# Two transformer stacks on one core: values computed token by token in all layers, and the memory layers' scores as three f32r products

## What is computed

```python
# layer 0 of the first stack ("in_e"): one projection, then three attentions
z = h @ w_in_e[i]                  # queries, keys, values, gates of 8 + 8 heads of 64
a_out = nsa_attention(...)         # compressed + selected + windowed branches, 2 key/value heads
b_out = swa_sink_attention(...)    # band of 128, with sinks, 2 key/value heads

# both layers of the second stack: attention over 256 memory tokens
def memory_cross_attention(h, m, w_q, w_kv, w_o):
    q = (h @ w_q).reshape(bsz, seq, MEM_HEADS, MEM_HEAD_DIM)       # 4 heads of 256
    k, v = jnp.split(m @ w_kv, 2, axis=-1)
    s = jnp.einsum("bqhd,bkhd->bhqk", q, k) * (MEM_HEAD_DIM ** -0.5)
    p = jax.nn.softmax(s, axis=-1).astype(v.dtype)
    o = jnp.einsum("bhqk,bkhd->bqhd", p, v).reshape(bsz, seq, D_MODEL)
    return o @ w_o
```

## Time and profile before

| what | us |
|---|---|
| median of 3 runs (lowest, highest) | 2790.49 (2789.91, 2791.82) |
| the profiled execution | 2792.47 |
| its span, from first to last instruction | 2790.7 |
| PE busy in the span | 2727.5 (98%) |
| POOL, ACT, DVE busy | 1272.4, 1103.4, 1024.8 |

### The profile page before, as it was taken

One profiled execution on the slowest core, in us unless ns is written; L12 is line 12 of the kernel. 1 busy time (PEld: TensorE's weight loads), 2 busy tenths in 40 slices (PEclk: granted clock), 3 DMA queues, 4 the chain that ended last, 5 costly groups with the idle time before them and its releaser, 6 DMA issues.

```text
span 2790.7 us, 38079 instructions
## 1 busy us (share of the span) xinstructions
PE 2727.5 (98%) x13618; PEld 2232.3 (80%) x13618; DVE 1024.8 (37%) x1935; ACT 1103.4 (40%) x1796; POOL 1272.4 (46%) x713
## 2 busy tenths in 40 slices
PE   9999999999999999999999999999999999999997
PEld 7767888888867888888868888888887798888886
DVE  6664322115453322105545235222047652422202
ACT  7665332335564323223155334232237453433321
POOL 4544444444454444444435534444444463454442
PEclk9999999999999999999999999999999999999999
DMA  5301223233301222332313312322322341132231
GB/s 186 106 2 39 98 90 101 100 101 102 99 31 58 97 98 98 99 104 72 113 46 111 131 46 76 103 92 98 105 84 93 103 151 46 61 113 98 91 108 65
DMA packets 69221, 252.06 MB, mean 90 GB/s; under 512 B 7680, under 2 KB 7936, under 8 KB 68864
## 3 DMA queue, kind: packets, MB, share of 16 engines
q1 hardware_dynamic: 68112, 247.43, 26.8%
q10 hardware_dynamic: 1008, 3.28, 0.4%
HBM read 248.58 MB, written 2.10 MB: 90 GB/s over the span
## 4 chain that ended last, share of the span: by engine, by line
PE 88%; DVE 6%; ACT 3%; issue 2%; DMA 1%; POOL 0%; DVEq 0%; SPq 0%; POOLq 0%; ACTq 0%
PE ps L587 25%; PE ps L589 25%; PE ps L588 25%; PE ps L767 3%; PE ps L802 3%; PE ps L788 2%; PE ps L697 1%; PE ps L699 1%; PE ps L698 1%; DVE ps L1941 1%; DVE x L1945 1%; DVE xl L1602 1%; DVE pr L1686 1%; POOL w_lo L502 0%; ACT pr L1185 0%
## 5 line engine op out<-in xcount | busy, mean ns | idle before, releaser
L502 POOL TENSOR_TENSOR w_lo<-w_raw,w_hi 128x1024 fp32r<-128x1024 f32 x460 | 1108.7, 2415 | 1293.9 <-ACT w_hi L1112 1291.1
L587 PE MATMUL ps<-xh,w_hi 128*128 128x512 f32 x2284 | 894.7, 392 | 7.5 <-DVE xl L1602 2.8
L589 PE MATMUL ps<-xh,w_lo 128*128 128x512 f32 x2284 | 889.0, 389 | 0.0
L588 PE MATMUL ps<-xl,w_hi 128*128 128x512 f32 x2284 | 888.9, 389 | 0.0
L1112 ACT ACTIVATE w_hi<-w_raw 128x1024 fp32r<-128x1024 f32 x462 | 485.8, 1056 | 522.5 <-PE ps L589 488.7
L587 PEld LDWEIGHTS ps<-xh,w_hi 128*128 128x128 f32 x2284 | 428.7, 188 | 104.0 <-issue 8.7
L589 PEld LDWEIGHTS ps<-xh,w_lo 128*128 128x128 f32 x2284 | 428.7, 188 | 90.0
L588 PEld LDWEIGHTS ps<-xl,w_hi 128*128 128x128 f32 x2284 | 428.8, 188 | 89.0 <-issue 1.2
L587 PE MATMUL ps<-hh,w_hi 128*128 128x512 f32 x704 | 273.9, 389 | 0.0
L588 PE MATMUL ps<-hl,w_hi 128*128 128x512 f32 x704 | 273.9, 389 | 0.0
L589 PE MATMUL ps<-hh,w_lo 128*128 128x512 f32 x704 | 273.9, 389 | 0.0
(11 more groups left out here) (293 smaller groups left out, 3036.1 us busy)
## 6 DMA issues: line engine op xcount, KB each, us to landing
w_raw<-weights_in SPq DMA_DIRECT2D x462, 512.0 KB, 3.3
x<-x_in SPq DMA_DIRECT2D x4, 512.0 KB, 7.4
mem<-mem_in ACTq DMA_DIRECT2D x2, 1024.0 KB, 5.1
x_out<-x SPq DMA_DIRECT2D x4, 512.0 KB, 2.6
rope<-rope_in SPq DMA_DIRECT2D x1, 512.0 KB, 10.4
tab<-tables_in ACTq DMA_DIRECT2D x2, 256.0 KB, 3.1
tab<-tables_in SPq DMA_DIRECT2D x1, 384.0 KB, 10.8
small<-small_in ACTq DMA_DIRECT2D x1, 326.5 KB, 4.5
```

What stands on the lines that cost most here:

```text
L502: nc.gpsimd.tensor_tensor(w_lo[:, slot], w_raw[:, slot], w_hi.bitcast(f32)[:, slot], ALU.subtract).then_inc(lo_ready, 1)
L587: nc.tensor.matmul(dst, w_hi[:, slot, w], hi, start=first, stop=False)
L588: nc.tensor.matmul(dst, w_hi[:, slot, w], lo, start=False, stop=False)
L589: return nc.tensor.matmul(dst, w_lo[:, slot, w], hi, start=False, stop=last)
```

## The change

1. **Layer 0's values.** The 17 tiles become 14: tiles 2 to 4 (values) go, all others move up by three, so rotated tiles are now 2 to 12 and the gates 13. The hidden layer's chunks still follow tiles 5 to 12. Three new chunks at the end hold the 384 value columns (`first_values`): here the tokens are the stationary side and the weights the moving one, 4 token tiles x 8 inputs x 3 products of 384 columns, cut where a chunk ends. The transposes and the fillers go; the scores of steps 0 and 1 and the first compressed scores are put between the value chunks. To scale them DVE computes the inverse norms as columns (`inverse_rms_columns`) right after tile 0, and ACT takes their root (`root_rows`) before it goes on.
2. **Memory values** likewise: 8 chunks of 2 token tiles with 512 moving columns instead of 8 tiles with 256 and 16 transposes; the columns of inverse norms are computed in the preceding linear layer (two more small f32 matmuls on PE).
3. **Memory scores**: DVE scales a key or query tile in its bank, ACT copies it out rounded (`kh_x`, `qh_x`), DVE subtracts (`kl_x`, `ql_x`) and only then frees the bank. The scores are three f32r products over these parts instead of one f32 product.
4. The compressed branch's hooks in layer 0's attention are listed one by one; the second block's scores come one step later and its transposes one step earlier.

```diff
-V_CHUNKS = {"qkv": 8, "ab_in": 4}
+V_CHUNKS = {"in_e": 3, "qkv": 8, "ab_in": 4, "xkv0": 8, "xkv1": 8}
...
# memory scores
-                    qk = [(q_x[:, 2 * h + c, tokens(t)], k_x[:, 2 * h + c, :]) for c in range(2)]
+                    qk = [(q[:, 2 * h + c, tokens(t)], k[:, 2 * h + c, :]) for c in range(2)
+                          for q, k in ((qh_x, kh_x), (ql_x, kh_x), (qh_x, kl_x))]
...
# layer 0's head on PE
-            keep_busy(4, IDLE_BANK)
-            pe.wait_ge(proj_ready, projs.n)
-            transpose_values(z_v0, 3)
...
+            def first_values():
+                c0 = in_e_chunk(TILES["in_e"] - 1) + 1
+                pe.wait_ge(evac_done, TILES["in_e"] - 2)
+                for v in range(V_CHUNKS["in_e"]):
+                    slot = (c0 + v) % RING
+                    pe.wait_ge(lo_ready, c0 + v + 1)
+                    for t in range(TB):
+                        if v == 0 and t == TB - 1:
+                            pe.wait_ge(cmp_hid, 1)
+                        for k, cols, w in value_pieces(v):
+                            bank, xs = ps[:, 3 + t, cols], (slice(None), k, tokens(t))
+                            nc.tensor.matmul(bank, xh[xs], w_hi[:, slot, w], start=k == 0, stop=False)
+                            nc.tensor.matmul(bank, xl[xs], w_hi[:, slot, w], start=False, stop=False)
+                            last = nc.tensor.matmul(bank, xh[xs], w_lo[:, slot, w], start=False, stop=k == KT - 1)
...
+                    if v == 0:
+                        second_layer()
+                        turn_gates()
...
+                    if v < BEGUN0:
+                        scores(U0, pairs_seen.n, v)
+                    if v == 1:
+                        cmp_scores(0)()
...
# layer 0's head on ACT
                 if m == 0:
                     root()
+                    root_rows()
...
-                if 5 <= m < 16:
+                if 2 <= m < 13:
-                    swap_halves(rot0[:, m % 2, 1], src, g)
...
# memory layers on ACT
-                    if 1 <= m <= KT:
+                    if m:
                         renormed_in_bank(m - 1, f"cross_pre{e}")
+                    act.wait_ge(qk_scaled, n_.qk.next())
+                    A(kh_x[:, m], ps[:, g % 4, 0:MEM], ACT.Copy).then_inc(qk_hi, 1)
...
# memory layers on DVE
-                    scaled(k_x[:, m] if m < 8 else z_vx[:, m - 8], bank, MEM, rstd_m).then_inc(evac_done, 1)
+                    scaled(bank[:, 0:MEM], bank, MEM, rstd_m).then_inc(qk_scaled, 1)
...
+                    dve.wait_ge(qk_hi, n_.qk.next())
+                    V.tensor_tensor(kl_x[:, m], bank[:, 0:MEM], fp(kh_x)[:, m], ALU.subtract).then_inc(evac_done, 1)
...
-                    scaled(q_x[:, m], bank).then_inc(evac_done, 1)
+                    scaled(bank, bank).then_inc(qk_scaled, 1)
+                    dve.wait_ge(qk_hi, n_.qk.next())
+                    V.tensor_tensor(ql_x[:, m], bank, fp(qh_x)[:, m], ALU.subtract).then_inc(evac_done, 1)
```

More of the change, by code:

```diff
@@ L39 @@
 FIRST_SUM = 5
[L40 to L41 removed]
+PROJ_AB = 14 + 16
+PROJ_REC = PROJ_AB + 21 + 8 + 8
 LINEARS = [
@@ L57 @@
     _c += _m * _q
-    _g += {"rec": 28, "cmp": 0}.get(_name, _m - V_CHUNKS.get(_name, 0))
+    _g += {"rec": 28, "cmp": 0, "xkv0": 12, "xkv1": 12}.get(_name, _m - V_CHUNKS.get(_name, 0))
 N_CHUNKS = _c
@@ L74, in cmp_chunk, with value_pieces @@
     return CMP_AFTER + 1 + 2 * q
+def value_pieces(v):
+    at, pieces = v * CW, []
+    while at < (v + 1) * CW:
+        k, a = divmod(at, V0_COLS)
+        n = min(V0_COLS - a, (v + 1) * CW - at)
+        pieces.append((k, slice(a, a + n), slice(at - v * CW, at - v * CW + n)))
+        at += n
+    return pieces
 REC = [("u", 4), ("u", 5), ("u", 6), ("l", 0), ("u", 7), ("l", 1), ("g", 0), ("g", 1), ("l", 2), ("l", 3),
@@ L744, in broadcast_rows @@
                 last.then_inc(rstd_ready, 1)
[L746 to L753, removed]
-                        last = nc.tensor.transpose(ps[:, bank, tokens(kb)], z[:, j, tokens(kb)], ident[:])
-                    last.then_inc(vt_ready, 1)
             def scores(steps, s0, s):
@@ L878, in _ @@
                         last.then_inc(chunk_done, 1)
-            sum_squares()
+            sum_squares_and_rows()
             pe.wait_ge(const_in, CONST_DMAS * 16)
-            for m in range(FIRST_TILES, 17):
+            for m in range(FIRST_TILES, TILES["in_e"]):
                 g, c = BANK0["in_e"] + m, in_e_chunk(m)
@@ L1169, in swap_halves @@
                 last.then_inc(swap_ready, 1)
-            def copy_values(dst, n):
-                act.wait_ge(vt_ready, n_.vt.next())
-                bank = ps[:, 4 + (n_.vt.n - 1) % 4, :]
-                A(dst, bank.rearrange("p (k c) -> p k c", c=dst.shape[-1]), ACT.Copy).then_inc(vt_copied, 1)
             def split_mix(g, hi, pairs):
@@ L1305, in _ @@
             highs = FIRST_TILES + 2
-            for m in range(17):
+            for m in range(TILES["in_e"]):
                 g = BANK0["in_e"] + m
@@ L1444, in memory_attention @@
                         root()
+                    act.wait_ge(qk_scaled, n_.qk.next())
+                    A(qh_x[:, m], ps[:, g % 4, :], ACT.Copy).then_inc(qk_hi, 1)
                 attention(UX, {})
@@ L2277, in _stream @@
     first = np.empty((17 + CMP_CHUNKS, P, CW), np.float32)
-    for m in range(17):
+    for m in range(TILES["in_e"]):
         first[in_e_chunk(m)] = by_tile[m]
+    first[17 + CMP_CHUNKS - V_CHUNKS["in_e"]:] = values.reshape(P, -1, CW).transpose(1, 0, 2)
     for q in range(CMP_CHUNKS):
```

254 lines of the change are left out of this document (141 added, 113 removed).

## The result

| what | before | after |
|---|---|---|
| median of the runs, us (lowest, highest; runs) | 2791.82 (2789.91, 2792.82; 9) | 2798.33 (2793.90, 2801.21; 9) |
| the profiled execution, us | 2792.47 | 2795.47 |
| its span | 2790.7 | 2793.7 |

The ratio of after to before is 1.0023, 95% interval [1.0014, 1.0032]: the change makes the kernel slower by 6.5 us, a little more than what can be told from no change. The forecast was 2790 in a range up to 2798. The profiled execution is only 3.0 us longer than that of before; the other 3.5 us of the median are in executions that are not in this trace, and the spread tells of them: 7.3 us over nine runs, where before had 2.9.

A forecast was written before the change was run, and what follows sets the result against it. PE, busy for 98% of the span, was taken as the bound. 2792.5 − 0.9 (layer 0's head) − 2 x 0.5 (memory layers) + 1.6 (clock) = 2792.2 profiled, 2790.2 against the median: 2790 us, range 2779 to 2798.

The forecast's parts named there:

- Layer 0, the early part: Layer 0's head up to tile 7: late chunks make tile 6 begin at 50.9 and tile 7 at 63.25, +9.3 us.
- Layer 0, the rest: Layer 0's head: three tiles go (−16.3), three value chunks come (+17.5), the stretch to step 8 shrinks (−11.4): −10.2 us.
- a step 8 later than 151: Layer 0's attention, forecast at 148.5: later than 151 would mean dearer value pieces or DVE still delaying the first steps.
- The clock: New PE idle stretches ahead of tiles 6 and 7 may halve the clock: +1.5 to 2 us, 1.6 in the sum.
- slower, by the clock: Falls of 3.3 us each ahead of tiles 6 and 7 and at memory attention's start give 2798 us; chance .12.
- The sign that the clock would be below 1 between 46 and 66: Layer 0 around tiles 6 and 7: the profile after would show the granted clock below 1 between 46 and 66 us.
- Memory layers: Both memory layers: less PE work, mostly given back in waits for DVE and ACT, −0.5 us each.
- Slower, by DVE in the memory layers: Added subtraction costs 1.2 us, DVE turns 4.0 and more, 3 us a layer: 2796, or 2799 with another fall; chance .07.
- The first two rivals: Two faster cases, layer 0's delay absent or halved (2779 or 2784 us) and everything hidden (2770 us); chance together .27.
- a head without the stall: Layer 0's 9.3 us loss does not come or is halved: 2779 or 2784 us; chance .23.
- all hidden: Head −10.2, each memory layer −3.6 − 1.3, no clock loss: 2770 us; chance .04.
- the stall: Layer 0's head: PE idles some 4.6 us ahead of tile 6, and tile 7 begins 9.3 us later than before.

The follow-up runs named there:

- both profiles of the changed kernel: The changed kernel as first measured, median 2798.33 us, and run once more unedited, median 2797.46 us, ratio 1.0022 to the kernel before.
- head by head: Changed kernel with the memory scores written as six products of the first head, then six of the second: median 2791.48 us, ratio 1.0002.
- The kernel with fewest waits: Changed kernel with hidden copy and chunk 9 rounding earlier, norm columns at tile 8, memory heads in turn, four fillers before memory scores: median 2781.19 us.

## Why the prediction was wrong

It forecast no change, 2790 us; the median is 2798.33, slower by more than the measurement's doubt and 0.3 us outside the range. Of the 8.1 us between 2790.2 and 2798.33, 1.3 is the median of before, which the forecast took from three runs (2790.49) and which is 2791.82 over nine. Another 3.3 is in the traces: 2795.47 measured against 2792.2 forecast, made of +3.4 in layer 0, +1.2 in the memory layers and −1.3 in stages that the change doesn't touch. The last 3.5 us is in the executions with more time at half clock. Step by step:

- **Layer 0, the early part: right.** Forecast of tile 6 and 7: 50.9 and 63.25; measured 51.04 and 62.98, and the chain through ACT, POOL and DVE agrees at each of its steps to 0.3 us.
- **Layer 0, the rest: this is the step that failed.** The sum took the value chunks at 17.5 us of PE work and gave them no wait. Value chunk 0 waits 2.35 us for a DVE copy behind a rotation that POOL stretches, which is the mechanism that the part before had used for tile 7, with the same rows, and had not carried on to the end of the tiles. Taking the copy forward removed this wait, 2.6 us with the slow matmul behind it. A second term was too small: without the wait the three chunks took 6.0, 7.1 and 5.8 us, 18.95 and not 17.5. Pieces of 128 columns come .103 us apart on average (123.96 to 124.58 for six) and not .09, near the upper bound that was taken from the transposes, and those of 384 columns .18 and not .173. The price of 81 ns that the prediction cited beside it from the Trainium skill ("TensorE: Matmul & The Clock Gate", section "Back-to-back issue gap") is not what these pieces cost here. Added up, the prediction's own terms put step 8 at 148.9 (it wrote 148.5); it began at 152.57. Of the 3.6 us, 2.35 is the wait, 1.45 the pieces and .8 a later end of the tiles (111.2 instead of 110.4, with the fall at 62.5); the steps behind the chunks took .95 less than their terms. The prediction had named a step 8 later than 151 as a sign, and for it the pieces or DVE in the first steps; the wait inside the chunk was neither.
- **The clock: right mechanism, mis-sized.** The prediction charged 1.6 us, for the waits ahead of tiles 6 and 7 alone. A fall takes 1.7 us or 3.4 (nothing between in 14 profiles), and the one ahead of tile 6 is mostly free. What was missed is that the waits that the kernel before has too can be followed by a fall in one execution and not in the next: the fall at 202.5 stands at a wait of 1.95 us that was 1.97 before without one, and in other executions it fell at 117, 147, 1605 and 2325. The changed kernel has five more waits of 2 us and over (tiles 6 and 7, value chunk 0, the first scores of each memory layer; that of tile 6 shrinks to 1.50 behind a fall), and so more places. On the other side, its sum took the fall at 140 out of layer 0 as if it belonged to that kernel; all three profiles with the old head do have one there (3.4, 3.4 and 1.7 us). This is the rival "slower, by the clock", given .12: it named tiles 6 and 7 and the first memory scores, and decided from the third fall. The sign that the clock would be below 1 between 46 and 66 was there in part: from 62.5 in the first trace, from 49 and again from 62.5 in the second.
- **Memory layers: −0.5 forecast, +0.3 measured in the first, −0.1 in the second.** Every wait came as told (2.45 us in `xkv0` against 2.5; 2.20 ahead of the scores; steps 2.3 apart). `xkv` to `xq` gained .36 and not .95. Each of the five waits makes the first matmul behind it slow as well (in `xkv0` the next one starts .33 us after it at 1537.33, where .23 is usual), which the sum left out; that this makes up the difference was not tried.
- **Slower, by DVE in the memory layers:** did not happen; the turns are 3.56 us, the subtraction .41.
- **The first two rivals** (a head without the stall, all hidden) fell: in both profiles of the changed kernel the stall is there.

By the kernels with one part each, in medians, about 4.3 us of the loss is layer 0's and 2.0 the memory part's, the latter not clear of no change. How often the clock falls behind a given wait stays open beyond the counts given: one profile shows one execution.

## What to carry to other kernels

- When an engine's list is stretched by a neighbour in one place of a sum, ask at each later point of the same list what stands behind it. Here one copy of .4 us was queued behind a rotation of 6 us, and moving it was worth 2.6 us.
- A new wait of PE costs its length and a chance of 1.7 or 3.4 us behind it. With fillers in a wait whose length is fixed (the first memory scores) the clock did not fall in four cases, at no cost; in one whose length varies (tile 7) they cost what they might have saved.
- Where two heads share a step and the next step waits for the first of them, finish one head and then the other: 1.7 us a layer with plain f32 scores, 2.9 with three f32r products. Cheaper matmuls alone had brought nothing there.

## What the runs showed of the hardware

- In 14 profiled executions each fall of PE's granted clock from 1.0 to 0.50 (2.4 to 1.2 GHz) took 1.7 or 3.4 us from PE, by the sum over its stretches, with a wait of PE of 1.2 us or more shortly ahead of it or in it. In each of two places (2125 to 2150 and 2187 to 2217) 13 of the 14 had one, elsewhere some had and some had not. The last 30 us, where PE has little left to do, are not counted.
- Executions of one kernel differ with their mean granted clock: the changed kernel took 2793.9 us at 0.995 and 2801.2 at 0.992, head by head 2786.8 at 0.996 and 2795.9 at 0.991. The kernel with fewest waits took 2779.9 to 2783.2.
- A fall ahead of a wait for another engine was free: tile 6 began at 51.04 with a fall at 22.5 (wait 1.50) and at 51.20 without it (wait 4.63).
- DVE operations of 128x512 f32 between SBUF tiles took .67 to .70 us where they met no `w_lo` of POOL (209 of them in the changed kernel's trace), and up to 2.9 us beside one.
